# A hybrid decoder layer on eight cores: the mixer recorded as steps that interleave three token tiles, with the residual kept in DRAM

## The reference

```python
for l in range(DEPTH):                                   # DEPTH = 1
    h = h + 0.5 * _swiglu(_rmsnorm(h, ffn1_norm[l]), ffn1_wg[l], ffn1_wu[l], ffn1_wd[l])   # D_FF 2816
    h = h + _mixer(h, mem, positions, ...)
    h = h + 0.5 * _swiglu(_rmsnorm(h, ffn2_norm[l]), ffn2_wg[l], ffn2_wu[l], ffn2_wd[l])
return _rmsnorm(h, final_norm)
...
def _mixer(h, mem, positions, ...):
    u = _rmsnorm(h, mix_norm)
    z = u @ w_in
    cq, ckv, krope, gq, gk, gv, ga, gr, xq, gz = _split_cols(z, IN_WIDTHS)
    o_mla = _mla(cq, ckv, krope, positions, ...) @ mla_w_o      # 8 heads, causal, softmax
    o_gla = _gla(gq, gk, gv, ga, gr, ...) @ gla_w_o             # 4 heads, chunked linear attention with decay
    o_x = _cross(xq, _rmsnorm(mem, mem_norm), x_w_kv) @ x_w_o   # 4 heads, 256 memory tokens
    gates = jax.nn.sigmoid(gz.reshape(B, S, N_BRANCH, D) + gate_bias)
    merged = gates[:, :, 0] * o_mla + gates[:, :, 1] * o_gla + gates[:, :, 2] * o_x
    return merged @ w_out
```

## Time and profile before

| | |
|---|---|
| median of three runs | 1954.29 us (1943.86 to 2145.74) |
| the profiled execution | 1967.71 us |
| its span on the slowest core (core 0) | 1966.7 us; all cores 1937.1 to 1966.7 us |
| busy share of the span | PE 88%, DVE 52%, ACT 34%, POOL 3% |
| matmul instructions recorded | 7714 |
| chain that ended last | PE 80%, ACT 7%, DVE 5%, issue 4%, DMA 3% |
| HBM | 204.00 MB read, 35.39 MB written |

### The profile page before, as it was taken

The page is one execution under the profiler, slowest core; times in us unless marked ns, Lnnn a source line. Parts: engine busy times, 40 slices in busy tenths (PEclk is TensorE's granted clock), DMA queues, the critical chain, the costliest instruction groups (busy, mean ns, idle before and its releaser), DMA issues.

```text
span 1966.7 us, 23970 instructions; the slowest of 8 cores (1937.1 to 1966.7 us)
## 1 busy us (share of the span) xinstructions
PE 1725.2 (88%) x7714; PEld 773.3 (39%) x7868; DVE 1014.5 (52%) x1718; ACT 669.7 (34%) x1014; POOL 60.0 (3%) x119
## 2 busy tenths in 40 slices
PE   2999995999987689867997889968899999999995
PEld 0444443344434234423442334423344444444442
DVE  3767772554555334432444334532348555666567
ACT  3411111001125642556334862658543111111124
POOL 1000001000000000000000000000000000000000
PEclk9999997788989799987998999979999999999998
DMA  9388877245232035600462014312253211122104
GB/s 224 62 101 100 105 108 101 37 59 74 53 126 87 30 97 162 187 26 33 134 222 78 27 61 165 117 33 103 83 143 54 43 33 33 33 50 48 33 1 171
DMA packets 49512, 168.91 MB, mean 86 GB/s; under 512 B 6816, under 2 KB 9264, under 8 KB 48432
## 3 DMA queue, kind: packets, MB, share of 16 engines
q0 software_dynamic: 13424, 55.55, 20.2%
q1 hardware_dynamic: 35968, 111.81, 17.5%
HBM read 204.00 MB, written 35.39 MB: 122 GB/s over the span
## 4 chain that ended last, share of the span: by engine, by line
PE 80%; ACT 7%; DVE 5%; issue 4%; DMA 3%; SPq 0%; ACTq 0%; DVEq 0%; POOLq 0%
PE ps_all L433 80%; ACT sa L459 2%; DMA hS<-x 2%; ACT hS L459 2%; DMA ring<-f 1%; ACT sa L897 1%; DVE hS L471 1%; DVE ntm L471 1%; ACT L459 1%; DVE om L466 1%; DVE sb L466 1%; ACT sa L908 0%; DVE hS L466 0%; DVE og L471 0%; ACT hS L482 0%
## 5 line engine op out<-in xcount | busy, mean ns | idle before, releaser
L433 PE MATMUL ps_all<-B,ring 128*128 128x512 bf16 x2760 | 638.6, 388 | 23.0 <-DMA ring<-f 17.5
L471 DVE SCALAR_TENSOR_TENSOR hS<-ps_all,hS 128x512 f32<-128x512 f32 (+1 forms) x744 | 457.1, 682 | 41.9 <-PE ps_all L433 40.6
L433 PE MATMUL ps_all<-sb,ring 128*128 128x512 bf16 (+1 forms) x1787 | 427.0, 389 | 15.7 <-DVE sb L471 6.1
L433 PEld LDWEIGHTS ps_all<-B,ring 128*128 128x128 bf16 x2816 | 279.9, 100 | 369.2 <-issue 84.3
L459 ACT ACTIVATE sa<-ps_all 128x512 f32<-128x512 f32 (+2 forms) x256 | 145.1, 569 | 790.8 <-PE ps_all L433 758.8
L433 PE MATMUL ps_all<-ntm,ring 128*128 128x512 bf16 x1310 | 328.7, 396 | 32.1 <-DVE ntm L471 11.2
L466 DVE TENSOR_TENSOR sb<-sa,ps_all 128x512 bf16<-128x512 f32 x176 | 120.4, 687 | 361.5 <-PE ps_all L433 354.7
L433 PEld LDWEIGHTS ps_all<-sb,ring 128*128 128x128 bf16 x1824 | 182.5, 100 | 238.0 <-issue 51.4
L433 PEld LDWEIGHTS ps_all<-ntm,ring 128*128 128x128 bf16 x1344 | 133.8, 101 | 203.1 <-issue 63.0
L471 DVE SCALAR_TENSOR_TENSOR sa<-sa,ps_all 128x512 f32<-128x512 f32 x96 | 65.6, 687 | 132.1 <-PE ps_all L433 110.6
L433 PE MATMUL ps_all<-sb,B 128*128 128x512 bf16 (+3 forms) x313 | 91.8, 367 | 34.3 <-ACT sa L897 18.3
(11 more groups left out here) (99 smaller groups left out, 973.6 us busy)
## 6 DMA issues: line engine op xcount, KB each, us to landing
ring<-wb SPq DMA_DIRECT2D x112, 512.0 KB, 4.0
ring<-f POOLq DMA_DIRECT2D x66, 512.0 KB, 6.8
wb<-wm POOLq DMA_DIRECT2D x28, 512.0 KB, 17.2
ring<-wb SPq DMA_DIRECT2D x48, 256.0 KB, 3.7
hS<-x SPq DMA_DIRECT2D x16, 512.0 KB, 30.8
spill<-hS SPq DMA_DIRECT2D x4, 2048.0 KB, 8.9
hS<-spill SPq DMA_DIRECT2D x16, 512.0 KB, 5.7
outT<-hS SPq DMA_DIRECT2D x16, 512.0 KB, 2.8
```

The lines of the kernel that those rows point to most:

```text
L433: i = e.matmul(_ap(o), lhsT=_ap(l), rhs=_ap(r), start=st, stop=sp)
L471: f.add([("dve", lambda e: e.scalar_tensor_tensor(out=_ap(out), in0=_ap(in0), scalar=_ap(scalar), in1=_ap(in1), op0=op0, op1=op1), c_dve(o ...
```

## The change

The mixer is no longer recorded tile by tile. Its work is cut into lists of small units with a weight each, and `weave` records two lists in proportion. Step t interleaves the attention of tile t with the list made of the merge of tile t-1, GLA and cross-attention of tile t, and norm and projections of tile t+1. The first projections stand alone before step 0, the last merge alone after step 3; the second half's norms of tiles 0 to 2 are recorded inside that last merge.

To make room, each tile's residual is stored to DRAM when the first half has finished it and fetched again for the norm, for the merge and for the second half, in pieces of 256 KB. `D2` takes 26 of the 32 residual slots; the other six hold a second set of `ntm` and `om` tiles (in the rows these are named hS). `A2` shrinks to 6 and `A1` to 13 tiles. Attention uses PSUM banks 0 to 2 for scores and 3 for outputs, one exponential per bank instead of per pair; everything else in the steps uses banks 4 to 7. The softmax division becomes copies and a DVE reciprocal per pair of heads.

In the first half, the weights of group g+1 are recorded before group g's side work, the norms stand inside group 0, x comes in pieces of 256 KB, and the memory's weights and the query weights `uq` get their own buffers. The planner gets a rule for ACT: rather than switch the activation table, take a ready operation that needs no switch, up to 120 recording numbers away.

```diff
@@ schedule
-                    cand = (free[e], a[0], e)
+                    s = a[0]
+                    if e == "act" and ops[s].table is not None and table not in ops[s].table:
+                        near = [q for q in a if not done[q] and q < s + 120 and
+                                (ops[q].table is None or table in ops[q].table)]
+                        if near:
+                            s = min(near)
+                    cand = (free[e], s, e)
...
-    A2 = Pool([T(f.sb(f"sa{i}", [128, TT], F32)[:], f"sa{i}") for i in range(8)])
-    A1 = Pool([T(f.sb(f"sb{i}", [128, TT], BF16)[:], f"sb{i}") for i in range(15)])
-    D2 = Pool([hslot[s][c] for s in (2, 3) for c in range(8)])
+    A2 = Pool([T(f.sb(f"sa{i}", [128, TT], F32)[:], f"sa{i}") for i in range(6)])
+    A1 = Pool([T(f.sb(f"sb{i}", [128, TT], BF16)[:], f"sb{i}") for i in range(13)])
+    D2 = Pool([hslot[s][c] for s in range(4) for c in range(8)])
...
@@ ffn
+        nxt = load(0)
         for g in range(NG):
-            wg, wu, wd = wload(w_d[g, 0], 8), wload(w_d[g, 1], 8), wload(w_d[g, 2], 2)
+            wg, wu, wd = nxt
             for t in tiles:
+                if g == 0:
+                    norm(t)
...
+            if g + 1 < NG:
+                nxt = load(g + 1)
             side(g)
@@ memory_kv
+        for i, (hnd, tiles) in enumerate(((om_h, o_mla0), (ox_h, o_x), (nt_h[:, 0:4, :], nM[0:4]), (nt_h[:, 4:8, :], nM[4:8]))):
+            v = R(tiles[0], hnd[:, :, :].rearrange("p a b -> p (a b)"))
+            f.dma("pool", v, xw_d[i], outs=tiles[1:], nbytes=1048576)
...
@@ gla_units
-            actf(sq.bf()[:, 0:TT], po, AF.Square, scale=128 ** -0.5)
+            cp(oc, po)
+            actf(sq.bf()[:, 0:TT], oc, AF.Square, scale=128 ** -0.5)
...
@@ attention_units
+        def u_full(hh, kc):
+            p = bank(BA)
+            score(hh, p, kc, 0)
+            PT = AH.get()
+            actf(PT, p, AF.Exp, scale=SC)
+            pv(hh, kc, PT, 0)
+            AH.put(PT)
...
+            cp(st["X"][num, :], PO[num, :])
+            cp(st["Y"][num, :], PO[den, :])
+            if hh % 2:
+                X, Y = st["X"], st["Y"]
+                f.add([("dve", lambda e: e.reciprocal(out=Y.ap, in_=Y.ap), 3.3)], outs=[Y], ins=[Y])
+                tt(om[hh // 2], X, Y, ALU.mult)
...
@@ merge_units
+                h = st["h"][c]
+                py = proj(w_, c2 * 128, 128, st["m"], bank(banks))
+                stt(h, py, 0.5, h, ALU.mult, ALU.add)
+                if not last:
+                    store(t, c, h)
...
+    def weave(a, b, lead):
+        ta, tb = sum(w for w, _ in a), sum(w for w, _ in b) * lead
+        da = db = 0.0
+        a, b = list(a), list(b)
+        while a or b:
+            if a and (not b or da / ta <= db / tb):
+                w, u = a.pop(0)
+                da += w
+            else:
+                w, u = b.pop(0)
+                db += w
+            u()
...
+    for _, u in next_units(0, hslot[0]):
+        u()
     for t in range(NT):
...
-        mixer_tile(t, hslot[slot_of[t]], before_out)
+        f.mark(f"step{t}")
+        b = (merge_units(t - 1, BB) if t else []) + gla_units(t) + (next_units(t + 1) if t + 1 < NT else [])
+        weave(attention_units(t), b, 0.95)
+    f.mark("merge3")
+    m = merge_units(NT - 1, BALL, last=True)
...
+    for i, (_, u) in enumerate(m):
+        u()
+        if i in (4, 7, 10):
+            norm2((i - 4) // 3)
```

More of the change, by code:

```diff
@@ L30, in __init__, with alias @@
         self.r = []
+        self.al = []
+    def alias(self, *others):
+        for o in others:
+            self.al.append(o)
+            o.al.append(self)
     def __getitem__(self, idx):
@@ L130, in add @@
                 continue
-            if t.w is not None:
-                deps.add(t.w)
-                raw.add(t.w)
+            for u in (t, *t.al):
+                if u.w is not None:
+                    deps.add(u.w)
+                    raw.add(u.w)
             if t.psum and t.r:
@@ L139, in add @@
                 continue
-            if t.w is not None:
-                deps.add(t.w)
-            deps.update(t.r)
+            for u in (t, *t.al):
+                if u.w is not None:
+                    deps.add(u.w)
+                deps.update(u.r)
         deps.discard(seq)
@@ L522, in build_program @@
     for t in order1:
[L523 to L526, removed]
+        for c in range(8):
+            f.dma("sp", hslot[t][c], x_d[t][:, c * TT:(c + 1) * TT], nbytes=262144)
     memset(ones, 1.0)
@@ L597, in rmsnorm, with ffn, load @@
         A2.put(rstd)
-    def ffn(w_d, hT, tiles, side, done):
+    def ffn(w_d, hT, tiles, side, done, norm):
         pending = [None]
+        def load(g):
+            return wload(w_d[g, 0], 8), wload(w_d[g, 1], 8), wload(w_d[g, 2], 2)
         def down(wd, a, t, last):
@@ L639, in memory_kv @@
     def memory_kv():
-        memf = [A2.get() for _ in range(4)]
+        memf = [VS.get() for _ in range(4)]
         for i in range(4):
@@ new lines, in build_program, with halves @@
+    BA, BB, BALL = (0, 1, 2), (4, 5, 6, 7), tuple(range(8))
+    PO = psum[3]
+    def halves(tiles):
+        out = []
+        for u in tiles:
+            for j in range(2):
+                out.append(T(u.bf().ap[:, j * TT:(j + 1) * TT], f"{u.name}_{j}"))
+                out[-1].alias(u)
+        return out
+    for s_ in (*hslot[2][0:6],):
+        D2.free.remove(s_)
+    nMix = [nM, halves(hslot[2][0:4])]
+    o_mla = [o_mla0, halves(hslot[2][4:6])]
+    nMix, o_mla = [nMix[1], nMix[0]], [o_mla[1], o_mla[0]]
@@ L714, in mixer_tile, with gla_units @@
+    def gla_units(t):
         par = t % 2
-        units = []
         st = {}
+        n_ = nMix[t % 2]
         def u_gates():
@@ L932, in mixer_tile, with merge_units, u_r @@
-        A1.put(*cqn)
-        A1.put(*qh)
-        fill(len(units))
-        f.mark(f"merge{t}")
-        for half in range(2):
+                units.append((0.65, lambda hh=hh: query(hh + 2)))
+            units += [(0.45, lambda hh=hh, kc=kc: u_full(hh, kc)) for kc in range(4 * t)]
+            units.append((1.1, lambda hh=hh: u_diag(hh)))
+            units.append((0.0, lambda hh=hh: u_out(hh)))
+        return units
+    def merge_units(t, banks, last=False):
+        st = {}
+        n = nMix[t % 2]
+        pl = A2 if last else D2
+        src = [o_mla[t % 2], [o_gla[:, i, :] for i in range(4)], o_x]
+        def u_r(half):
@@ L971, in mixer_tile, with u_res, u_out @@
+        def u_res():
+            st["h"] = hslot[3] if last else [D2.get() for _ in range(8)]
+            for c in range(8):
+                fetch(t, c, st["h"][c])
+        def u_out(cg):
             w_ = mload("wout", cg, 8)
```

425 lines of the change are left out of this document (221 added, 204 removed).

## The result

The changed kernel took 1877.99 us, median of three runs (1852.87 to 1903.26), against 1954.29 us. The ratio, taken from the faster executions alone (1850.04 and 1852.87 us now, 1943.86 and 1954.29 us before), is 0.950, with a 95% interval of 0.939 to 0.961: 5% faster. The forecast was 1809 us with a range of 1750 to 1890.

The account below looks back on a forecast made before the run. TensorE, 80% of the span, was taken as the bound, with only its idle time and slow clock to win. First half 535, mixer 785 and second half 488 gave 1808 us of span, 1809 of time; range 1750 to 1890.

Parts of the forecast that it names:

- The stall: First half: TensorE's 17.5 us wait for a weight load goes, as loads stand one group ahead; −17.5 us.
- The 0.81 stretch: First half, core 0: the granted clock of 0.81 after the stall until 480 us does not return; −23 us.
- The start: First 60 us: 17 us more DMA for extra loads, offset by earlier first gates; 0, with −10 to +5 us.
- Tile 0: First projections and attention of tile 0: the old 117 us stage plus 10 for tile 1's projections; 127 us.
- The three steps: Steps 1 to 3, attention woven with merge, GLA and projections: 348 us beside the merge, 218 without; 566 in all.
- the tails: Second part of each woven step, with no merge beside it: 174 us of work at rate 0.80; 218 us.
- the first parts: Part of each woven step while the merge lasts: 337 us of work at rate 0.97; 348 us.
- The reciprocal: 16 DVE reciprocals in attention, 0.68 to 1.22 us each, beside TensorE's work; still covered at the planner's 3.3 us.
- (a): Woven steps run no better than the best old attention stage, rate 0.68: 751 us instead of 566, 1994 total; chance 0.07.
- (b): The clock falls to 0.81 where TensorE becomes dense, in 440 us of merge-bound stretches: +94 us, 1903 total; chance 0.08.
- (c): Late ring loads: each of 160 mixer loads 0.7 us late and uncovered costs 112 us, 1921 total; chance 0.07.
- (d): Latencies in the steps stay: tails at 0.68 (256 us), first parts at 0.92 (366), 1865 total; inside the forecast's 0.78.

Follow-up runs that it names:

- e1: The changed kernel with its four xw loads and two uq loads recorded later, out of the first 70 us; ratio 0.944 to the kernel before.
- e3: The changed kernel with all four first norms recorded ahead of the feed-forward loop, as before the change; ratio 0.946 to the kernel before.
- e5: The changed kernel with xw and uq loads later, x in 512 KB pieces and the first norms ahead of the loop; 1817.85 us, ratio 0.934.
- e11: e5 with a tile of its own for each of the 16 rotary-key copies, so none waits for the one before; 1800.64 us, ratio 0.927.
- e4: The changed kernel with each merge recorded ahead of the next tile's attention instead of woven with it; ratio 0.957 to the kernel before.
- e12: The changed kernel with each of the 16 reciprocals done twice, the second result unused; ratio 0.961 to the kernel before.
- e2: The changed kernel with x loaded in 16 pieces of 512 KB instead of 32 of 256 KB; ratio 0.947 to the kernel before.

## Why the prediction was right, and where it was not

*The stall.* Right. No PE wait for ring<-f in the first half; between 250 and 350 us what is left is the 5.9 us pause for the memory's norm. Behind it six cores had a granted clock of 0.98 to 1.00.

*The 0.81 stretch.* The 23 us taken as won on core 0 had no cause behind them. I saw the stretch behind a long stall and counted on its going with the stall; on two cores it came back behind a pause of 5.9 us that all eight cores have, and their tile 0 began at 597.0 us against 566.7 on core 4, 30 us later. As the sum itself says, core 2 had no such 23 us to win; without the stretch the first half ended at 548.7 us before (core 2) and at 558.2 now (core 4). The Trainium skill ("TensorE: Matmul & The Clock Gate", section "Seeing it yourself") says that a peak-current limit sets the whole die to 13/16 of the clock once a third core runs dense matmuls. The level agrees with the 0.81, the rest doesn't: core 2 stood at 1.00 in the same microseconds as core 1, and all eight cores were dense.

*The start.* This step failed. I priced the extra loads at 17 us of DMA, then let the shorter queue of norm matmuls pay for it, and wrote 0 (−10 to +5). The price was near: e1 gives back 14 us. The credit against it was not there. The earlier gates did not come earlier (56.3 us, against 44.6 on core 2 of the kernel before), since six norm matmuls of the second tile stand before them and their x lands later with the extra loads. The count of 88 feed-forward matmuls by the time x is in was a sum of TensorE's own work, and by 72 us there were 40: the gates of each later tile also wait for a norm whose squares, logarithm and products stand in the in-order queues of ScalarE and VectorE behind other tiles' squares. The pause that I expected near 60 to 70 us for the last x came from 71.6 to 77.2 us, and for such a norm. And I had given the smaller pieces no price at all. e1 to e3 measure 14, 8 and 8 us, e5 all three together 34; on core 4 the first half ended 23 us after the forecast.

*Tile 0.* Right, 128 against 127, and by its own reason: it is a serial head with nothing beside it. e11 shows that 11 us of it were the copies waiting for one another, which I had listed as "16 rotary-key DMAs in a row at 1.8 us each" without asking why they were in a row.

*The three steps.* The sum is right (569 against 566), each step within its 180 to 195 us (187, 193, 189), PE 0.90, 0.93 and 0.98 busy. The reason given for it is right only in part. I named the weave with the merge as what lifts the rate, and kept the tails at 0.80 for the removed serial head. By e4 the weave is worth 15 us; the rest comes with the projections that moved (59, which include some 20 us of norm waits that the kernel before did not have) and the cheaper end of a head (42 without cover, of which 12 are copies that the new plan left uncovered), and the new attention stage alone runs at 0.78, 0.81 and 0.87 (355, 419 and 406 units of 0.219 us in 100, 113 and 102). The tails stood at 0.74 and not 0.80 (174 us of work in 234, 16 more than forecast), the first parts at 1.00 and not 0.97 (337 in 335, 13 less). That the two errors cancel is luck.

*Last merge and second half.* 586 against 580. The second half has waits of 8.0 and 5.0 us on core 4 for a norm, ahead of 418 dense us; the sum had none. Both traces hold 7868 matmuls where the prediction has 7,860; the work is the same in both, as it says.

*The reciprocal.* Bounds too low: 0.68 to 1.22 us, by rows of other operations, against 3.35, which the planner's number had right. I had said that 53 us would still be covered. Of a second 53 us, e12 shows, two thirds are; the first were not taken away alone.

*The rivals.* (a) fell: no step ran below 0.86. (b) fell for the steps, where the first parts stand at 1.00. (c) fell: PE waits for ring<-wb add up to 1.9 us on core 4. (d) came true by half for the tails, which took 234 us, between the forecast's 218 and its 256; the first parts, at 1.00, were far from its 0.92.

## What to carry to other kernels

Cost the start of a kernel by its queues as well as by its bytes: for each first matmul, list what stands ahead of it on every in-order engine and when that can end. A part that shortens a latency can be worth much less once another part covers it (the division: 42 us uncovered, 6 covered), so undo parts one on top of the other before saying which brought the gain, and read the waits of each run, since a new plan also moves work that the edit did not touch. And where small transfers run one after the other, look first at whether they depend on one another or only share a name.

## What the runs showed of the hardware

- A VectorE reciprocal of 128 x 512 f32 takes 3.35 us, 4.9 times the 0.68 us of an ordinary two-operand pass on the same shape.
- A granted clock of 0.81 from 340 to 505 us came to the cores 0 and 1 of the traced execution, while the other six, with the same instructions and the same 5.9 us pause ahead of it, stood at 0.98 to 1.00. In the kernel before it came to the cores 0, 1, 6 and 7; in an execution of the changed kernel of 1850.04 us no core's mean clock is below 0.968. What decides it is not known from these runs.
- With x in 32 pieces of 256 KB, SP was issuing x until 63 us; with 16 of 512 KB and no other edit, until 31 us (e2). With the 32 pieces and the xw and uq loads moved away it was 46 us (e1).
